# Three whole feature tiles in the first part of each FFN stage in place of four

## The reference

```
h += 1/2 * SwiGLU_1(RMSNorm(h))        FFN stage 0, d_ff = 2816
u  = RMSNorm(h);  P = u @ w_in         gated DeltaNet (4 heads of 128) and a conv branch of 512 channels
h += concat(DeltaNet, conv) @ w_out
h += 1/2 * SwiGLU_2(RMSNorm(h))        FFN stage 1, d_ff = 2816
y  = RMSNorm(h)
SwiGLU(x) = (silu(x @ w1) * (x @ w3)) @ w2
```

## Time and profile before

| | us |
|---|---|
| median of 3 runs (1206.69 to 1208.52) | 1207.96 |
| the profiled execution | 1213.22 |
| its span | 1211.1 |
| TensorE (PE) busy | 1194.6 |
| VectorE (DVE) busy | 787.3 |
| ScalarE (ACT) busy | 515.8 |
| GpSimd (POOL) busy | 75.2 |

### The profile page before, as it was taken

How to read it: one execution, slowest core, us unless ns; L and a number is a source line. 1 busy time by engine, 2 the same in 40 slices (tenths; PEclk the granted TensorE clock), 3 DMA queues, 4 the chain that set the end, 5 groups by cost and what they waited for, 6 DMA issues and landing times.

```text
span 1211.1 us, 21067 instructions
## 1 busy us (share of the span) xinstructions
PE 1194.6 (99%) x8832; PEld 1167.1 (96%) x8832; DVE 787.3 (65%) x1155; ACT 515.8 (43%) x820; POOL 75.2 (6%) x58
## 2 busy tenths in 40 slices
PE   9999999999999999999999998999999999999997
PEld 9999999999999998999989897999999999999997
DVE  6897565767566644666447786537785667675764
ACT  6345343535344542333443444433444344353355
POOL 0000000000000300000125210220000000000003
PEclk9999999999999999999999999999999999999999
DMA  5322212222223422111600002322123131222112
GB/s 189 127 86 73 105 61 96 88 105 79 96 79 109 127 73 79 60 53 54 125 4 1 1 2 88 117 84 88 53 105 109 72 116 62 96 104 105 70 71 78
DMA packets 39212, 99.68 MB, mean 82 GB/s; under 512 B 12112, under 2 KB 15568, under 8 KB 39120
## 3 DMA queue, kind: packets, MB, share of 16 engines
q1 hardware_dynamic: 38064, 96.00, 23.5%
q10 hardware_dynamic: 1056, 2.36, 0.5%
HBM read 92.91 MB, written 5.44 MB: 81 GB/s over the span
## 4 chain that ended last, share of the span: by engine, by line
PE 96%; DVE 2%; ACT 1%; issue 1%; DMA 0%; POOLq 0%; DVEq 0%; POOL 0%; SPq 0%
PE ps L839 34%; PE ps L806 21%; PE ps L755 20%; PE ps L951 12%; PE ps L1329 4%; PE ps L719 1%; PE ps L1135 1%; PE ps L1343 1%; PE ps L1241 1%; ACT x_hi L1411 1%; DVE w_lo L1906 1%; DVE h L1968 1%; PE ps L921 0%; PE ps L973 0%; DMA h<-x_t 0%
## 5 line engine op out<-in xcount | busy, mean ns | idle before, releaser
L839 PE MATMUL ps<-x_hi,s_hi 128*128 128x296 f32 (+1 forms) x576 | 171.2, 297 | 0.2
L839 PE MATMUL ps<-x_hi,s_lo 128*128 128x296 f32 (+1 forms) x576 | 170.9, 297 | 0.0
L839 PE MATMUL ps<-x_lo,s_hi 128*128 128x296 f32 (+1 forms) x576 | 170.9, 297 | 0.0
L755 PE MATMUL ps<-x_hi,w_hi 128*128 128x296 f32 (+1 forms) x608 | 136.8, 306 | 0.3 <-DVE x_lo L1911 0.3
L755 PE MATMUL ps<-x_lo,w_hi 128*128 128x296 f32 (+1 forms) x608 | 133.0, 300 | 0.0
L755 PE MATMUL ps<-x_hi,w_lo 128*128 128x296 f32 (+1 forms) x608 | 132.5, 299 | 0.0
L839 PE MATMUL ps<-t_hi,s_hi 128*128 128x296 f32 (+1 forms) x432 | 128.3, 297 | 0.0
L839 PE MATMUL ps<-t_hi,s_lo 128*128 128x296 f32 (+1 forms) x432 | 128.1, 297 | 0.0
L839 PE MATMUL ps<-t_lo,s_hi 128*128 128x296 f32 (+1 forms) x432 | 128.0, 296 | 0.0
L2005 DVE TENSOR_TENSOR s_lo<-s_sum,s_hi 128x1024 fp32r<-128x1024 f32 x72 | 88.2, 1225 | 44.2 <-ACT s_hi L1398 41.5
L839 PEld LDWEIGHTS ps<-x_hi,s_hi 128*128 128x128 f32 x576 | 108.4, 188 | 0.6 <-issue 0.6
(11 more groups left out here) (316 smaller groups left out, 2558.8 us busy)
## 6 DMA issues: line engine op xcount, KB each, us to landing
raw<-weights SPq DMA_DIRECT2D x150, 512.0 KB, 3.4
raw<-weights SPq DMA_DIRECT2D x16, 384.0 KB, 3.5
S<-states SPq DMA_DIRECT2D x1, 2048.0 KB, 11.8
new_state<-S ACTq DMA_DIRECT2D x1, 2048.0 KB, 6.9
y_t<-h SPq DMA_DIRECT2D x4, 336.0 KB, 2.3
h<-x_t SPq DMA_DIRECT2D x4, 296.0 KB, 4.7
h<-x_t SPq DMA_DIRECT2D x2, 592.0 KB, 7.5
raw<-weights SPq DMA_DIRECT2D x4, 256.0 KB, 5.2
```

The lines of the kernel that those rows point to most:

```text
L755: last = nc.tensor.matmul(ps[:, slot if out is None else out, half, 0:w_half], w[:, slot, k, :], x[:, k, a:a + w_half], start=(k == 0 and ...
L839: last = nc.tensor.matmul(out, w[:, k, :], x[:, k, :], start=(start and k == 0 and r == 0), stop=(k == KT // 2 - 1 and r == 2), skip_group ...
```

## The change

The list of parts is 3, 4, 4, 3, 4, 4 in place of 4, 4, 3, 3, 4, 4. So three tiles of a stage are made whole and nineteen by sevenths (before: four and eighteen). What follows from it: the first part's down units begin at unit 6 of the stage, so their slots turn by two; the loads of the first part are written as loops over `DIRECT`, by which the query history's load comes one pair earlier; the turns of the weight sets go one further, so the last two down units of stage 0 lie in `raw` and not in `raw2`, and the first two `U_GLU` loads wait for their splits.

```diff
-PARTS = [4, 4, 3, 3, 4, 4]
+PARTS = [3, 4, 4, 3, 4, 4]
...
             if part.at == 0:
-                return w_hi[:, v], w_lo[:, v]
+                return w_hi[:, (part.down + v) % 4], w_lo[:, (part.down + v) % 4]
...
-            load_pair(2)
-            load_pair(4)
-            load_pair(6)
+            for u in range(2, 2 * DIRECT, 2):
+                load_pair(u)
             sp.dma_start(hq[:], hist_q).then_inc(hist_in, 16)
-            load_pair(8)
-            load_pair(10)
+            for u in range(2 * DIRECT, 2 * DIRECT + ADDS, 2):
+                load_pair(u)
             load_parts(0)
             for j in range(2):
-                sp.wait_ge(w_lo_ready, U_GLU - 2)
+                sp.wait_ge(w_lo_ready, U_GLU - 1 + j)
                 sp.dma_start(raw[:, j], weights[U_GLU + j]).then_inc(raw_in[j], 16)
```

## The result

The changed kernel takes 1224.09 us (median of 4 runs, 1223.38 to 1225.59) against 1208.24 (4 runs): ratio 1.0128, 95% interval 1.0113 to 1.0143. It is slower by 15.8 us; 12.4 were forecast. The range of 1214 to 1224 is +6.0 to +16.0 us on the median of 1207.96 from which it was worked out, so the measured difference lies just inside its upper end. Later comparisons have 17 or 23 runs of the kernel before, with medians of 1209.6 to 1209.9. The changed kernel was not run in them; if its time carries over, some 14.4 us is the better size.

The account below looks back on a forecast made before the run. TensorE's matmul count bounds the kernel while VectorE stays ahead, barely so in the first parts. Gain -3.2, stalls +9.7 and +5.1 make +11.6, with the clock +12.4: 1220.4 us from the median of 1207.96, range 1214 to 1224.

Parts of the forecast that it names:

- The count: TensorE, both stages: 12 matmuls fewer a stage, 8808 in place of 8832, gaining 3.2 us.
- The first stall: Stage 0's first part: TensorE waits 3.1 us for the third tile's g_lo; no such stall in the second stage.
- the 9.7 us: Stage 0's first part: TensorE's total standing time, from g_lo to the first tile by sevenths.
- The adds: First parts: VectorE's adds reach add 5 late; TensorE waits at outputs 5 to 7 and 2.6 us at the sevenths.
- The edits at nothing: Weight sums, later GLU loads, earlier query history load, other parts' orders: all put at zero cost.
- the margins of 0.5 and 0.2 us: Kernel before, first and second stage: time between VectorE's add and TensorE's start on the first tile by sevenths.
- The sum: Whole kernel: -3.2 + 9.7 + 5.1 = +11.6 us, with the clock +12.4.
- The clock: Half-clock spells after new stalls: none, or one for each stage, 3.4 us; half of one taken, 0.85.
- The third rival: Both stages: stalls as forecast and a half-clock spell paid behind both, +15.0 us, 1223.0; chance 21%.
- a spell within the down products is free: First parts: its 1.7 us is less than the following stall, as TensorE waits for the adds anyway.
- Rivals 1, 2 and 4: 1: no new stall, 1204.8, 5%; 2: only the g_lo wait, 1207.9, 4%; 4: one stage only stalls, 1214.5, 8%.
- rival 5: Whole kernel: the change does not do what it says, so the matmul count would not be 8808; chance 1%.

Follow-up runs that it names:

- e9: Kernel before with three whole tiles in stage 1 only and a second VectorE order in both stages: 1211.49 us, ratio 1.0024 to the kernel before.
- e6: Changed kernel with TensorE repeating matmul pairs (90 matmuls more) where it would stand in its stalls: 1218.4 us, 5.7 us under the changed kernel.
- e5: Changed kernel with, in stage 0, half sums T3 and T1 and T3's low part moved behind the third tile's g_lo: 1224.15 us against 1224.09.
- e4: Changed kernel with VectorE's adds earlier in the first part and two TensorE waits moved to their own products: 1215.77 us, 8.3 us under the changed kernel.
- e7: Changed kernel with one more, unused VectorE subtraction before add 2 in each stage's first part: 1226.92 us, 2.8 over the changed kernel.
- e1: Changed kernel with parts 4, 3, 4, 3, 4, 4, so four whole tiles again: 1209.85 us against 1209.74 for the kernel before, ratio 1.0002.
- e8: Kernel before with one more, unused VectorE subtraction in each stage's first part: 1211.58 us against 1209.72, ratio 1.0023.
- e2: Kernel before with three whole tiles in stage 0 only, stage 1 unchanged: 1220.55 us, ratio 1.0089 to the kernel before.

## Why the prediction was right

**The count.** 8808 matmuls at an unchanged pitch, and 3.2 us to gain: e9's C and e6's B minus A (342.06 against 323.96 before, 18.1 us for the 132 matmuls that come back) bear out 0.1367 and 0.1322 us each.

**The first stall.** 3.1 us at the third tile's g_lo were forecast, 2.96 measured, none in stage 1. It was treated as a part of the 9.7 us, not as an addition; e5 shows that this is how it is.

**The adds.** Add 5 was to start at 75.6 and the seventh at 76.35; they are at 75.83 and 76.75, and the first down product is 0.27 us later in this trace than in that of the kernel before. That the adds are what TensorE waits for, and the order of VectorE's queue what makes them late, is shown by e4 (the same work in another order, 8.3 us less) and e7 (1.3 us more work, 1.3 us more a stage). Stage 1: add 0 to add 5 16.28 us as forecast, the wait at the seventh 2.36 where 2.6 was said, at outputs 5 and 6 0.26 and 1.72 where 2.5 together with output 7 was said.

**The edits at nothing** were nothing (e1 for the later loads, the changed kernel's own trace for the rest), and the margins of 0.5 and 0.2 us were real (e8).

**The sum.** Stalls less gain were put at 11.6; at equal clock the difference is 11.3 (e6). The stages were put at +8.1 and +3.5; the traces have +7.9 in B without a paid spell (412.35 - 404.46), and D less its spell, as in e6, +3.3 (383.68 - 380.36).

**The clock** is the term that was mis-sized: 0.85 us was taken, 3.1 to 4.5 were paid (14.4 or 15.8 less 11.3). The third rival, a spell paid in each stage, 1223.0, had the size more nearly and was given 21%. Its mechanism is only in part what the runs show: in the changed kernel's profile one spell is paid, 1.5 us in stage 1, none in stage 0, and in e2's profile one in stage 0 too. Where the rest of the clock's share is paid is not shown; the prediction put nothing outside the first parts, and e6 gains there as well. The waits near 2 us in the earlier trace rows had a spell in two of three cases, and the change adds five waits of 1.7 us or more, so half a spell was too little. That a spell within the down products is free held for the changed kernel (the 0.36 us wait at output 5). So the mechanism and the sum of the stalls were right, and the clock term was under a third of what was paid.

Rivals 1, 2 and 4 are excluded by the waits, which come to 11.7 us where under 10 would have spoken against the forecast; rival 5 by the count.

## What to carry to other kernels

An engine that the page shows 65% busy can be 0.2 us from being the bound in one stretch: before you take work from the busiest engine, follow the in-order queue of the next one from its last idle moment to the last thing that the busiest engine waits for, and compare the two lengths. Waits that stand in one chain don't add up; the distance to its end does, and removing the longest of them can change nothing (e5). A stall also has a price in clock, which an experiment can take apart by keeping TensorE busy with repeated matmuls that change nothing. Check also that a control run still contains the edits it is to test: e1 turned most of them off with the fourth tile.

## What the runs showed of the hardware

Execution times of one kernel come in steps of 1.3 to 1.6 us that go with the mean granted clock: the kernel before took 1206.6 to 1207.3 at 0.997, 1208.0 to 1208.4 at 0.996, 1209.6 to 1210.3 mostly at 0.994, 1211.2 to 1211.7 at 0.993 and 1213.0 to 1213.2 at 0.991. One step is about one half-clock spell, which cost 1.5 us in stage 1 of the changed kernel (D 385.2 against 383.7 in e5 and e6, which have none there). In the changed kernel's stage 1 such a spell began behind a wait of TensorE of 2.36 us, and in e2 at the end of one of 2.35; in the changed kernel's stage 0 a wait of 2.35 us had none.
